# Five mixing products of an encoder block, multiplied by quarters with seven products of sums

## Chip, cores and metric

One core of one Trainium2 chip. The time is that of the device from the start to the end of one execution, in microseconds.

## What is computed

One layer of a hybrid encoder over 512 tokens of width 1024, all in float32. A Mamba-2 branch A and an S5 branch B leave `y_a` (512x1536, before its output matrix) and `y_b` (512x768, before its two). What the change touches is the mixing of the two:

```
A   = y_a @ w_out                                   # 1536 -> 1024
B   = (y_b @ w_glu_a) * sigmoid(y_b @ w_glu_b)      # 768 -> 1024, twice
mix = sigmoid(gate_a) * A + sigmoid(gate_b) * B
h   = LN(alpha * x + mix @ w_o)
out = LN(alpha * h + expert_choice_moe(h))          # 16 experts, 64 tokens each
```

## The kernel before

It is a program with semaphores written by hand, one instruction stream for each engine. The stages follow one another: input projections and gates, S5, the Mamba-2 loop over 4 groups and 4 token tiles, the mixing, the product with `w_o` with the first layer norm and the router, then 8 pairs of experts, whose weights (some 550 MB) stream from HBM.

**The mixing** is done in two halves of 512 output columns, each of three products: m = 0 and 3 with `w_glu_b`, m = 1 and 4 with `w_glu_a`, m = 2 and 5 with `w_out` in two weight slices. A product has four token tiles c (128 tokens); `mix_tile` (L1243) sums one tile in one PSUM bank over 6 (`w_glu`) or 12 (`w_out`) steps of 128 rows, each a matmul of 128x128 weights (tokens) by 512 columns. In float32 each such matmul stands in the trace as two weight loads and two matmul records. Product 0 runs partly inside the Mamba-2 loop; the loop `for m in range(6)` (L1286) runs the rest, 5 products after `y_transposed` of the last tile. `m_bank` (L301) gives products of odd and even m four banks each, so product m waits only for the readers of product m-2 (`before`, L1010).

**Readers.** ScalarE takes products 0 and 3 by tiles through a sigmoid to `sg_u`. VectorE (L1864 to L1882) multiplies products 1 and 4 with `sg_u` and the gate `sg[:, hf, 1]` into `mix`, and products 2 and 5 with the gate `sg[:, hf, 0]` into `tmix`, which it adds to `mix` (`mix_ready`). The gates `sg` come from HBM scratch (L464) once the last tile of branch A is transposed (`yt_copied`).

**After the mixing.** `mix_transposed` (L1302) transposes `mix` by token tiles, ScalarE copies them to `mixT`, `out_product` multiplies by `w_o`, VectorE adds the residual (L1901), and norm, router and the choice of tokens follow, with `max_ready` raised at L1910.

**SyncE's queue** works in the order of the code. `slices` (L391) loads weight slices into a ring of two places, `wring`; slice i waits by `released` for the last reader of slice i-2. In the mixing: slices FIRST_MIX+2.. are `w_out` (two), `w_glu_b`, `w_glu_a`, `w_out` (two), `w_o` (two). Behind them come `x_res` (L467), the first norm's rows `lnrow` (L469), then the expert weights (L471 on), which wait for `mix_ready` 2*TT, for free places of their ring, and (L480) for `max_ready` before they may go over `wring`.

## Time and profile before

| | us |
|---|---|
| median of 3 runs (2117.92 to 2119.32) | 2118.39 |
| the profiled execution | 2114.42 |
| its span in the trace | 2112.7 |
| TensorE busy in the span | 1934.8 (92%) |
| VectorE busy | 589.0 (28%) |
| mean granted TensorE clock | 0.956 of full |

The span is the part of the profiled execution that the trace covers. A share of busy time is a mean over stages with different limits; which engine sets the pace of a stage is read from that stage.

### The profile page before, as it was taken

The page shows a single profiled execution, that of the slowest core. Times are in us where ns is not written, and L with a number is a line of the kernel's source. Part 1 is how long each engine was busy: PE and PEld are TensorE (multiplying, and loading weights), DVE is VectorE, ACT ScalarE, POOL GpSimd, SP SyncE. Part 2 cuts the span into 40 slices and gives each one's busy share as a digit, 9 for nine tenths or more (in the row PEclk, how much of TensorE's full clock was granted, in tenths as well). Part 3 has the DMA queues.
Part 4 walks back from the last instruction along what each step waited for, and adds up shares of the span by engine and source line. Part 5 has one row for each costly group of instructions (what it writes and reads, how often), then busy time and mean ns, then how long its engine had stood idle before and what let it go on. Part 6 is the DMA issues. An engine that isn't in the chain of part 4 may idle for free.

```text
span 2112.7 us, 19729 instructions
## 1 busy us (share of the span) xinstructions
PE 1934.8 (92%) x8256; PEld 913.9 (43%) x8256; DVE 589.0 (28%) x1085; ACT 376.8 (18%) x680; POOL 252.3 (12%) x268
## 2 busy tenths in 40 slices
PE   8999999999999997999898898899888898988987
PEld 4656654466644454343343342343334333334332
DVE  6599757598711134001001001000000100100102
ACT  1444302289700021000000000000000000000001
POOL 1787400165300000000000000000000000000001
PEclk9999999999999998999999999899999999999999
DMA  5632313243332286999999999999999999999995
GB/s 147 137 96 60 106 35 127 70 124 120 105 140 89 88 354 250 418 426 429 427 425 430 428 424 429 428 425 428 428 425 428 429 426 428 427 427 427 429 426 216
DMA packets 92631, 638.13 MB, mean 302 GB/s; under 512 B 21452, under 2 KB 35200, under 8 KB 62336
## 3 DMA queue, kind: packets, MB, share of 16 engines
q1 hardware_dynamic: 79904, 628.99, 73.2%
q10 hardware_dynamic: 12640, 7.89, 1.2%
q8 instruction: 65, 1.06, 0.2%
q14 instruction: 22, 0.18, 0.0%
HBM read 626.98 MB, written 9.88 MB: 301 GB/s over the span
## 4 chain that ended last, share of the span: by engine, by line
PE 59%; DMA 29%; DVE 2%; ACT 2%; issue 0%; SPq 0%; DVEq 0%
PE ps L1000 58%; DMA arena<-in_w_e 29%; ACT arena L663 1%; ACT L663 0%; DVE arena L1925 0%; DVE arena L1923 0%; PE ps L1118 0%; DVE arena L2016 0%; DVE arena L1973 0%; PE ps L1181 0%; PE ps L1492 0%; PE ps L1235 0%; DVE arena L2010 0%; SPq L491 0%; PE ps L1311 0%
## 5 line engine op out<-in xcount | busy, mean ns | idle before, releaser
L1000 PE MATMUL ps<-arena 128*64 128x512 f32 (+8 forms) x7722 | 1869.1, 529 | 144.0 <-DMA arena<-in_w_e 106.7
L1000 PEld LDWEIGHTS ps<-arena 128*64 128x64 f32 (+2 forms) x7722 | 850.4, 162 | 1139.2 <-issue 1035.8
L663 ACT ACTIVATE arena<-ps 128x512 f32<-128x512 f32 (+5 forms) x278 | 152.3, 581 | 1614.6 <-PE ps L1000 916.0
L1982 DVE TENSOR_TENSOR arena<-arena,ps 128x512 f32<-128x512 f32 (+1 forms) x48 | 30.2, 644 | 566.7 <-PE ps L1000 566.6
L655 POOL TENSOR_TENSOR arena<-arena 128x1024 f32<-128x1024 f32 x3 | 7.1, 2352 | 1364.4 <-ACT arena L663 1364.4
L663 ACT ACTIVATE arena<-arena 128x128 f32<-128x128 f32 (+9 forms) x260 | 117.5, 510 | 76.3 <-DVE arena L1889 20.8
L1991 DVE TENSOR_TENSOR arena<-arena,ps 128x512 f32<-128x512 f32 x48 | 33.1, 690 | 335.9 <-PE ps L1000 335.9
L663 ACT ACT_TABLE_LOAD x74 | 94.9, 1283 | 23.0 <-issue 21.3
L1771 DVE SCALAR_TENSOR_TENSOR arena<-arena 128x512 f32<-128x512 f32 x80 | 63.5, 794 | 2.8
L1973 DVE TENSOR_TENSOR arena<-arena 128x512 f32<-128x512 f32 x8 | 5.6, 694 | 185.6 <-PE ps L1492 185.6
L615 POOL TENSOR_TENSOR arena<-arena 128x768 f32<-128x768 f32 x16 | 28.5, 1780 | 180.0 <-PE ps L1181 129.1
L1573 DVE TENSOR_TENSOR arena<-arena 128x320 f32<-128x320 f32 x48 | 28.4, 654 | 0.6
L509 POOL TENSOR_TENSOR arena<-arena 128x256 f32<-128x256 f32 x40 | 24.9, 655 | 4.3 <-ACT arena L663 3.3
L1879 DVE TENSOR_TENSOR arena<-ps,arena 128x512 f32<-128x512 f32 x8 | 5.5, 692 | 71.0 <-PE ps L1000 71.0
L605 POOL TENSOR_TENSOR arena<-arena 128x384 f32<-128x384 f32 x24 | 24.5, 1038 | 3.5 <-PE ps L1000 3.5
L616 POOL TENSOR_TENSOR arena<-arena 128x768 f32<-128x768 f32 x16 | 24.2, 1512 | 0.0
L1871 DVE TENSOR_TENSOR arena<-ps,arena 128x512 f32<-128x512 f32 x8 | 5.5, 691 | 65.4 <-PE ps L1000 38.5
L1458 PE MATMUL ps<-arena 128*128 128x128 f32 x176 | 23.4, 289 | 0.0
L1458 PEld LDWEIGHTS ps<-arena 128*128 128x128 f32 x176 | 21.9, 211 | 3.1 <-DVE arena L1982 3.1
L546 POOL TENSOR_TENSOR arena<-arena 128x512 f32<-128x512 f32 (+4 forms) x19 | 16.8, 886 | 41.9 <-DVE arena L1577 25.3
L647 POOL MEMSET arena<- 128x128 f32 x1 | 0.2, 204 | 176.8 <-PE ps L1311 176.8
L1768 DVE TENSOR_SCALAR arena<-arena 128x512 f32<-128x512 f32 x20 | 10.9, 546 | 36.1 <-ACT arena L663 36.1
(197 smaller groups left out, 686.2 us busy)
## 6 DMA issues: line engine op xcount, KB each, us to landing
arena<-in_w_e SPq DMA_DIRECT2D x120, 2816.0 KB, 28.8
arena<-in_w_e SPq DMA_DIRECT2D x80, 2048.0 KB, 28.4
arena<-in_w_e SPq DMA_DIRECT2D x16, 1408.0 KB, 21.2
arena<-in_w_in SPq DMA_DIRECT2D x9, 2048.0 KB, 8.6
arena<-in_w_e SPq DMA_DIRECT2D x16, 1024.0 KB, 31.3
arena<-cumulative_scratch SPq DMA_DIRECT2D x16, 768.0 KB, 5.1
arena<-in_w_in SPq DMA_DIRECT2D x5, 1536.0 KB, 6.8
arena<-in_w_out_ssd SPq DMA_DIRECT2D x4, 1536.0 KB, 6.7
```

Of the source, the lines that this page charges most:

```text
L509: n.done(eng.tensor_tensor(tmp[t], x, y, ALU.mult))
L546: n.done(pool.tensor_tensor(out[0], x[0], y[0], ALU.mult))
L605: pool.tensor_tensor(xw[:, d].rearrange("p (h w) -> p h w", h=HG), xs[:, c, GI * g:GI * g + GI].rearrange("p (h w) -> p h w", h=HG), last( ...
L615: pool.tensor_tensor(diff_f, cum_rows[:, i % 2, 0], last(cum[:, 0, c, h], P), ALU.subtract)
L616: pool.tensor_tensor(diff_b, cum_rows[:, i % 2, 1], last(cum[:, 1, c, h], P), ALU.subtract).then_inc(s.diff_ready, 1)
L663: return act.activation(out, in_, func, **kw)
L1000: return pe.matmul(out, lhsT, rhs, start=a, stop=z)
L1458: r = pe.transpose(ps[:, i, P * t:P * t + P], block[:, t, :], ident)
L1573: n.done(tt(tv[t], x, y, ALU.mult))
L1771: r = stt(cacc[:, j], raw[:, j, k:k + SEQ], conv_w[:, i, k:k + 1], cacc[:, j], ALU.mult, ALU.add)
L1982: tt(o, o, ps[:, i, 0:w], ALU.mult).then_inc(s.hid_ready, 1)
L1991: r = tt(o, o, ps[:, 6 + k % 2, :], ALU.add)
```

## The change

Product 0 stays as it was. Products 1 to 5 are each cut in quarters: 2x2 quarters of the tokens and the inner dimension on the left (`factors`, a), 2x2 quarters of the inner dimension and the columns on the right (b), 2x2 quarters of 256 tokens by 256 columns in the result. Where eight quarter products would do, seven products of sums are taken: VectorE makes four sums of each side beforehand (`lhs_term`, `rhs_term`), TensorE multiplies P1, P5, P6, P7, P2, P3, P4 (`mix_product`, each in one bank), ScalarE copies P1 to SBUF (`one`), and VectorE adds the seven to the four quarters of the result, in place in the banks (`first_sums`, `last_sum`). Products 1, 3 and 4 have a left side of 768 columns (GK = 3 steps of 128 in a quarter), 2 and 5 one of 1536 (OK = 6). The left sums are made once for `y_b` and once for `y_a`. The 35 products go around eight banks (`product_banks`), so a product waits for the readers of the one eight before it. `mix` and the sigmoid are then made by quarters, in the order of `quarters`. `w_o`'s two slices, and the slice behind each product, are asked for when the last product that reads the place is done, before the last of the seven; `lnrow` and `mixT` hold sums, so `lnrow` is loaded after `mix_ready` TT+3. Transposing of tiles 0 and 1 waits for three quarters, of tiles 2 and 3 for four. Outside the mixing, four semaphores of the S5 parameters (`lr_ready`, `theta_ready`, `tanh_done`, `sin_done`) become two that count to 2, and `before` goes.

```diff
@@ -298,7 +298,43 @@
-        m_bank = ((2, 3, 0, 4), (1, 5, 6, 7))
+        m_bank = (2, 3, 0, 4)
+        product_banks = (1, 5, 6, 7, 2, 3, 0, 4)
+        HALF, GK, OK = SEQ // 2, 3, 6
+        S = Space(arena, ring_at + 11640, top)
+        lhs_glu = S.take(4, GK, HALF)
+        rhs_glu = S.take(4, GK, HALF)
+        rhs_out = [S.take(OK, HALF) for _ in range(2)]
+        flat_rest = lambda x, rest: x.rearrange(rest)[:, OK * HALF:OK * HALF + 2 * HALF].rearrange("p (t w) -> p t w", t=2)
+        with_sixth = S.take(2, HALF)
+        with_fifth, one = flat_rest(mixT, "p a k t -> p (a k t)"), flat_rest(lnrow, "p a d -> p (a d)")
+        rhs_out += [lnrow.rearrange("p a d -> p (a d)")[:, 0:OK * HALF].rearrange("p (k t) -> p k t", k=OK),
+                    mixT.rearrange("p a k t -> p (a k t)")[:, 0:OK * HALF].rearrange("p (k t) -> p k t", k=OK)]
+        S = Space(arena, ring_at - TT * D_MODEL - 2 * 6 - TT * 4 - KT * P, ring_at)
+        lhs_out = [S.take(OK, HALF) for _ in range(2)] + [yT[:, 0:OK, HALF:SEQ], S.take(OK, HALF)]
+        terms_at = lambda m, k: 2 * k if m == 1 else 8 + 4 * (m - 1) + k
+        mix_at = lambda m, n: n if m == 0 else TT + 7 * (m - 1) + n
+        sums_at = lambda m, n: 7 * (m - 1) + n
+        mix_slice = lambda m: FIRST_MIX + m + (m > 2)
+        def factors(m):
+            y, nk, w = (yT, OK, [wring[:, (mix_slice(m) + j) % NW, 0:OK] for j in range(2)]) if m % 3 == 2 else (
+                ysT, GK, [wring[:, mix_slice(m) % NW, GK * j:GK * j + GK] for j in range(2)])
+            a = [[y[:, nk * k:nk * k + nk, HALF * r:HALF * r + HALF] for k in range(2)] for r in range(2)]
+            b = [[w[k][:, :, HALF * q:HALF * q + HALF] for q in range(2)] for k in range(2)]
+            return a, b
+        P1, P5, P6, P7, P2, P3, P4 = range(7)
+        def product(m, x):
+            return ps[:, product_banks[(7 * (m - 1) + x) % 8], :].rearrange("p (t w) -> p t w", t=2)
+        def quarter(buf, r, q):
+            return buf[:, 2 * r:2 * r + 2, HALF * q:HALF * q + HALF]
+        quarters = ((1, 1), (0, 0), (0, 1), (1, 0))
+        quarter_product = (P7, P2, P3, P4)
...
@@ -383,10 +419,14 @@
+                if i == FIRST_MIX:
+                    return s.mix_ps, TT
                 half, j = divmod(i - FIRST_MIX, 4)
+                m = 3 * half + min(j, 2)
                 if j == 2:
-                    return s.slice_used, half + 1
-                return s.mix_ps, TT * (3 * half + min(j + 1, 3))
+                    return s.mix_ps, mix_at(m, 4)
+                sp.wait_ge(s.terms_ready, terms_at(m, 4))
+                return s.mix_ps, mix_at(m, 6)
...
+            sp.wait_ge(s.mix_ready, TT + 3)
             for i, name in enumerate(("ln1_g", "ln1_b")):
...
@@ -898,14 +939,24 @@
-            for half in range(2):
-                m = 3 * half
-                for c in range(TT):
-                    act.wait_ge(s.mix_ps, TT * m + c + 1)
-                    if half:
-                        act.wait_ge(s.mix_read, TT)
-                        act.wait_ge(s.glu_done, TT)
-                    f(sg_u[:, c, :], ps[:, m_bank[m % 2][c], :], ACT.Sigmoid).then_inc(s.mix_sig, 1)
+            for c in range(TT):
+                act.wait_ge(s.mix_ps, c + 1)
+                f(sg_u[:, c, :], ps[:, m_bank[c], :], ACT.Sigmoid).then_inc(s.mix_sig, 1)
+            def first_product_copied(m):
+                act.wait_ge(s.mix_ps, mix_at(m, 1))
+                if m >= 2:
+                    act.wait_ge(s.quarter_sums, sums_at(m - 1, 5))
+                f(one, product(m, P1), ACT.Copy).then_inc(s.one_copied, 1)
+            for m in range(1, 4):
+                first_product_copied(m)
+            act.wait_ge(s.mix_read, TT)
+            act.wait_ge(s.glu_done, TT)
+            for i, x in enumerate(quarter_product):
+                act.wait_ge(s.quarter_sums, sums_at(3, 4 + i))
+                f(quarter(sg_u, *quarters[i]), product(3, x), ACT.Sigmoid).then_inc(s.mix_sig, 1)
+            for m in range(4, 6):
+                first_product_copied(m)
...
@@ -1237,19 +1281,56 @@
+            def mix_tile(c, w):
+                for kk in range(2 * GK):
+                    r = mm(ps[:, m_bank[c], :], ysT[:, kk, P * c:P * c + P], w[:, kk, :], kk == 0, kk == 2 * GK - 1)
+                r.then_inc(s.mix_ps, 1)
+            def taken(m, i):
+                if m == 0:
+                    return s.mix_sig, i + 1
+                return (s.mix_sig, TT + i + 1) if m == 3 else (s.mix_read, TT * (1, 2, 4, 5).index(m) + i + 1)
+            def mix_product(m, x, lhs, rhs):
+                n = lhs.shape[1]
+                for t in range(2):
+                    for k in range(n):
+                        r = mm(product(m, x)[:, t, :], lhs[:, k, P * t:P * t + P], rhs[:, k, :], k == 0, k == n - 1)
+                r.then_inc(s.mix_ps, 1)
+            def mix_products(m):
+                a, b = factors(m)
+                sa, tb = (lhs_out, rhs_out) if m % 3 == 2 else ([lhs_glu[:, j] for j in range(4)], [rhs_glu[:, j] for j in range(4)])
+                slice_wait()
+                if m >= 2:
+                    pe.wait_ge(*taken(max(m - 2, 0), 3))
+                mix_product(m, P1, a[0][0], b[0][0])
+                pe.wait_ge(s.terms_ready, terms_at(m, 1))
+                if m >= 2:
+                    pe.wait_ge(s.one_copied, m - 1)
+                mix_product(m, P5, sa[0], tb[0])
+                pe.wait_ge(s.terms_ready, terms_at(m, 2))
+                if m >= 2:
+                    pe.wait_ge(s.quarter_sums, sums_at(m - 1, 2))
+                mix_product(m, P6, sa[1], tb[1])
+                pe.wait_ge(s.terms_ready, terms_at(m, 3))
+                mix_product(m, P7, sa[2], tb[2])
+                if m % 3 == 2:
+                    slice_wait()
+                pe.wait_ge(*taken(m - 1, 0))
+                mix_product(m, P2, a[0][1], b[1][0])
+                pe.wait_ge(*taken(m - 1, 1))
+                if m == 1:
+                    pe.wait_ge(s.terms_ready, 7)
+                mix_product(m, P3, sa[3], b[1][1])
+                pe.wait_ge(s.terms_ready, terms_at(m, 4))
+                pe.wait_ge(*taken(m - 1, 2))
+                mix_product(m, P4, a[1][1], tb[3])
...
+                    mix_tile(c - (TT - 2), mix_w[0])
+            pe.wait_ge(s.z_silu, GROUPS * TT)
+            pe.wait_ge(s.g_ready, GROUPS * TT)
+            for c in range(2, TT):
+                mix_tile(c, mix_w[0])
+            y_transposed(GROUPS * TT - 1)
+            pe.wait_ge(s.yt_copied, 3 * GROUPS * TT)
+            pe.wait_ge(s.gate_ready, GROUPS * TT)
+            for m in range(1, 6):
+                mix_products(m)
             w_o = []
             def mix_transposed(c):
-                pe.wait_ge(s.mix_ready, TT + c + 1)
+                pe.wait_ge(s.mix_ready, TT + (3 if c < 2 else 4))
                 if c == 0:
-                    pe.wait_ge(*before(4, TT - 1))
+                    pe.wait_ge(s.one_copied, 5)
...
@@ -1861,25 +1937,95 @@
+            def lhs_term(m, k):
+                (a11, a12), (a21, a22) = factors(m)[0]
+                t = lhs_out if m % 3 == 2 else [lhs_glu[:, j] for j in range(4)]
+                x, y, op = ((a21, a22, ALU.add), (t[0], a11, ALU.subtract), (a11, a21, ALU.subtract), (a12, t[1], ALU.subtract))[k]
+                if k:
+                    dve.wait_ge(s.terms_ready, 2 * k if m == 1 else 8 + k)
+                tt(t[k], x, y, op).then_inc(s.terms_ready, 1)
+            def rhs_term(m, k):
+                (b11, b12), (b21, b22) = factors(m)[1]
+                t = rhs_out if m % 3 == 2 else [rhs_glu[:, j] for j in range(4)]
+                x, y = ((b12, b11), (b22, t[0]), (b22, b12), (b21, t[1]))[k]
+                i = mix_slice(m) + (1 if m % 3 == 2 and k else 0)
+                dve.wait_ge(slice_loaded[i % NW], 16 * (i // NW + 1))
+                if k:
+                    dve.wait_ge(s.terms_ready, terms_at(m, k))
+                tt(t[k], x, y, ALU.subtract).then_inc(s.terms_ready, 1)
+            def first_sums(m):
+                dve.wait_ge(s.one_copied, m)
+                dve.wait_ge(s.mix_ps, mix_at(m, 1 + P6))
+                tt(with_sixth, one, product(m, P6), ALU.add).then_inc(s.quarter_sums, 1)
+                dve.wait_ge(s.quarter_sums, sums_at(m, 1))
+                tt(with_fifth, with_sixth, product(m, P5), ALU.add).then_inc(s.quarter_sums, 1)
+                dve.wait_ge(s.mix_ps, mix_at(m, 1 + P7))
+                dve.wait_ge(s.quarter_sums, sums_at(m, 2))
+                tt(with_sixth, with_sixth, product(m, P7), ALU.add).then_inc(s.quarter_sums, 1)
+                dve.wait_ge(s.quarter_sums, sums_at(m, 3))
+                tt(product(m, P7), product(m, P7), with_fifth, ALU.add).then_inc(s.quarter_sums, 1)
+                dve.wait_ge(s.quarter_sums, sums_at(m, 4))
+            def last_sum(m, i):
+                x = quarter_product[i]
+                dve.wait_ge(s.mix_ps, mix_at(m, 1 + x))
+                tt(product(m, x), product(m, x), (one, with_fifth, with_sixth)[i - 1], ALU.add).then_inc(s.quarter_sums, 1)
+                dve.wait_ge(s.quarter_sums, sums_at(m, 4 + i))
+            def taken(m, i):
+                if m % 3 == 0:
+                    return
+                hf, o = m // 3, quarter(mix[:, :, 512 * (m // 3):512 * (m // 3) + 512], *quarters[i])
+                y = product(m, quarter_product[i])
+                if m % 3 == 1:
+                    dve.wait_ge(s.mix_sig, TT if not hf else TT + i + 1)
+                    tt(o, y, quarter(sg_u, *quarters[i]), ALU.mult).then_inc(s.mix_read, 1)
+                    dve.wait_ge(s.mix_read, 2 * TT * hf + i + 1)
+                    tt(o, o, quarter(sg[:, hf, 1], *quarters[i]), ALU.mult).then_inc(s.glu_done, 1)
+                else:
+                    if hf or i:
+                        dve.wait_ge(s.mix_ready, TT * hf + i)
+                    t = tmix.rearrange("p (t w) -> p t w", t=2)
+                    tt(t, y, quarter(sg[:, hf, 0], *quarters[i]), ALU.mult).then_inc(s.mix_read, 1)
+                    dve.wait_ge(s.mix_read, TT * (2 * hf + 1) + i + 1)
+                    dve.wait_ge(s.glu_done, TT * hf + i + 1)
+                    tt(o, o, t, ALU.add).then_inc(s.mix_ready, 1)
+            dve.wait_ge(s.ysT_ready, S5_W // P)
+            for k in range(4):
+                lhs_term(1, k)
+                rhs_term(1, k)
+            dve.wait_ge(s.yt_copied, 3 * GROUPS * TT)
+            for k in range(4):
+                lhs_term(2, k)
+            for m in range(1, 6):
+                first_sums(m)
+                if m == 1:
+                    dve.wait_ge(s.sg_loaded, 64)
+                taken(m, 0)
+                last_sum(m, 1)
+                taken(m, 1)
+                if m in (1, 4):
+                    rhs_term(m + 1, 0)
+                if m == 3:
+                    for k in range(3):
+                        rhs_term(4, k)
+                last_sum(m, 2)
+                taken(m, 2)
+                if m == 2:
+                    for k in range(4):
+                        rhs_term(3, k)
+                last_sum(m, 3)
+                taken(m, 3)
+                if m in (1, 4):
+                    for k in range(1, 4):
+                        rhs_term(m + 1, k)
+                if m == 3:
+                    rhs_term(4, 3)
```

## Rows read from the trace of the kernel before

**Rows 1.** The page: busy time of the engines, chain that ended last by engine
```profile
PE 1934.8 (92%) x8256; PEld 913.9 (43%) x8256; DVE 589.0 (28%) x1085; ACT 376.8 (18%) x680; POOL 252.3 (12%) x268
...
PE 59%; DMA 29%; DVE 2%; ACT 2%; issue 0%; SPq 0%; DVEq 0%
```

**Rows 2.** Chain that ended last, 560 to 840 us: start, us, what
```profile
590.61 144.47 PE ps L1000 x336
...
735.08 0.45 PE ps L1311 x4
...
737.85 13.74 PE ps L1000 x32
```

**Rows 3.** SyncE's queue: longest waits (total, times, longest), then its issues in order
```profile
SPq L480 <- DVE arena L1910: 56.3, 1, 56.3
...
737.50 82.47 SPq L488 DMA_DIRECT2D arena<-in_w_e  x16
...
807.51 12.46 SPq L488 DMA_DIRECT2D arena<-in_w_e  x6
```

**Rows 4.** Two stretches: us, busy PE, PEld, DVE, ACT, POOL, PEclk, DMA share, GB/s
```profile
784.00:807.50 23.50, 21.71 (x88) 12.20 (x87) 16.44 (x45) 7.98 (x12) 0.00 (x0) 1.00 0.01 2
...
807.50:2083.00 1275.50, 1134.52 (x5296) 469.00 (x5298) 90.59 (x152) 73.70 (x139) 0.00 (x0) 0.94 1.00 424
```

**Rows 5.** Groups of TensorE by form, 590.61 to 735.08 us
```profile
L1000 PE MATMUL ps<-arena 128*128 128x512 f32 x336 | 144.5, 592 | 1.0 <-ACT arena L663 1.0
```

**Rows 6.** The weight loads of the same stretch
```profile
L1000 PEld LDWEIGHTS ps<-arena 128*128 128x128 f32 x336 | 63.8, 190 | 81.1 <-issue 79.9 <-ACT arena L663 1.2
```

**Rows 7.** Loads beside 128x384 matmuls, 460.42 to 465.58 us
```profile
L1000 PEld LDWEIGHTS ps<-arena 128*128 128x128 f32 x16 | 3.0, 190 | 2.1
```

**Rows 8.** Matmuls of 128 columns, 934 to 943 us
```profile
L1000 PE MATMUL ps<-arena 128*128 128x128 f32 x64 | 7.9, 284 | 0.9 <-DVE arena L1973 0.9
```

**Rows 9.** Weight loads in order around two 256-column matmuls: start, us, line
```profile
894.29 0.14 PEld L1000 LDWEIGHTS ps<-arena 128*64 128x64 f32 x2 [0.29 <-issue]
...
894.72 0.58 PEld L1000 LDWEIGHTS ps<-arena 128*64 128x64 f32 x6 [0.29 <-issue]
...
895.59 0.14 PEld L1000 LDWEIGHTS ps<-arena 128*64 128x64 f32 x2 [0.29 <-issue]
```

**Rows 10.** VectorE by form, whole span: busy us, mean ns
```profile
L1871 DVE TENSOR_TENSOR arena<-ps,arena 128x512 f32<-128x512 f32 x8 | 5.5, 691 | 65.4 <-PE ps L1000 38.5 <-DMA arena<-gate_scratch 26.9
...
L1719 DVE TENSOR_TENSOR ps<-ps,arena 128x512 f32<-128x512 f32 x12 | 8.4, 700 | 0.4
```

**Rows 11.** VectorE in order, 530 to 640 us
```profile
545.32 0.95 DVE L1798 TENSOR_TENSOR arena<-arena 128x768 f32<-128x768 f32 x1
...
553.90 1.84 DVE L1798 TENSOR_TENSOR arena<-arena 128x768 f32<-128x768 f32 x1
...
577.12 0.42 DVE L1822 TENSOR_SCALAR arena<-arena 128x384 f32<-128x384 f32 x1
...
604.46 0.69 DVE L1871 TENSOR_TENSOR arena<-ps,arena 128x512 f32<-128x512 f32 x1 [26.91 <-DMA arena<-gate_scratch]
```

**Rows 12.** GpSimd in order, 530 to 740 us
```profile
551.05 8.13 POOL L643 COPY arena<-arena 128x512 f32<-128x512 f32 x6
...
736.02 0.20 POOL L647 MEMSET arena<- 128x128 f32 x1 [176.84 <-PE ps L1311]
```

**Rows 13.** DMA issues of 585 to 620 us: count, KB, us to landing
```profile
arena<-gate_scratch SPq DMA_DIRECT2D x4, 1024.0 KB, 8.7
...
arena<-in_w_out_ssd SPq DMA_DIRECT2D x2, 1536.0 KB, 11.2
```

**Rows 14.** DMA issues of the whole span
```profile
arena<-in_w_out_ssd SPq DMA_DIRECT2D x4, 1536.0 KB, 6.7
...
arena<-in_w_o SPq DMA_DIRECT2D x2, 2048.0 KB, 7.9
```

More of the change, by code:

```diff
@@ L691, in _ @@
             f(small[:, 0], par[:, :, 2, :], ACT.Exp).then_inc(s.step_exp, 1)
-            act.wait_ge(s.lr_ready, 1)
-            f(small[:, 3], small[:, 1], ACT.Tanh, scale=0.5).then_inc(s.tanh_done, 1)
-            act.wait_ge(s.theta_ready, 1)
+            act.wait_ge(s.exponent_ready, 1)
+            f(small[:, 3], small[:, 1], ACT.Tanh, scale=0.5).then_inc(s.tanh_sin_done, 1)
+            act.wait_ge(s.exponent_ready, 2)
             f(small[:, 5], small[:, 4], ACT.Sin)
-            f(small[:, 6], small[:, 4], ACT.Sin, scale=0.5).then_inc(s.sin_done, 1)
+            f(small[:, 6], small[:, 4], ACT.Sin, scale=0.5).then_inc(s.tanh_sin_done, 1)
             for c in range(S5_W // P):
@@ L1008, in slice_wait @@
                 return wring[:, i % NW]
-            def before(m, c):
-                sigmoids, products = (0, 3), (1, 2, 4, 5)
-                if m in sigmoids:
-                    return s.mix_sig, sigmoids.index(m) * TT + c + 1
-                return s.mix_read, products.index(m) * TT + c + 1
             pe.wait_ge(s.consts_ready, 7)
@@ L1236, in y_transposed @@
                 r.then_inc(s.yt_ps, 1)
-            nk = 6
             mix_w = []
-            def mix_tile(m, half, c, w):
-                lhs, halves = (yT, 2) if m % 3 == 2 else (ysT, 1)
-                for kk in range(nk):
-                    r = mm(ps[:, m_bank[m % 2][c], :], lhs[:, nk * half + kk, P * c:P * c + P], w[:, kk, :],
-                           half == 0 and kk == 0, half == halves - 1 and kk == nk - 1)
-                if half == halves - 1:
-                    r.then_inc(s.mix_ps, 1)
-                elif c == TT - 1:
-                    r.then_inc(s.slice_used, 1)
+            def mix_tile(c, w):
+                for kk in range(2 * GK):
+                    r = mm(ps[:, m_bank[c], :], ysT[:, kk, P * c:P * c + P], w[:, kk, :], kk == 0, kk == 2 * GK - 1)
+                r.then_inc(s.mix_ps, 1)
@@ L1283, in _ @@
                         mix_w.append(slice_wait())
-                    mix_tile(0, 0, c - (TT - 2), mix_w[0])
-            for m in range(6):
-                if m == 0:
-                    pe.wait_ge(s.z_silu, GROUPS * TT)
-                    pe.wait_ge(s.g_ready, GROUPS * TT)
-                if m == 1:
-                    y_transposed(GROUPS * TT - 1)
-                    pe.wait_ge(s.yt_copied, 3 * GROUPS * TT)
-                    pe.wait_ge(s.gate_ready, GROUPS * TT)
-                for half in range(2 if m % 3 == 2 else 1):
-                    w = slice_wait() if m else mix_w[0]
-                    for c in range(0 if m else 2, TT):
-                        if half == 0 and m >= 2:
-                            pe.wait_ge(*before(m - 2, c))
-                        mix_tile(m, half, c, w)
+                    mix_tile(c - (TT - 2), mix_w[0])
[8 more added lines that the diff above has]
+                mix_products(m)
             w_o = []
             def mix_transposed(c):
-                pe.wait_ge(s.mix_ready, TT + c + 1)
+                pe.wait_ge(s.mix_ready, TT + (3 if c < 2 else 4))
                 if c == 0:
-                    pe.wait_ge(*before(4, TT - 1))
+                    pe.wait_ge(s.one_copied, 5)
                 else:
@@ L1611, in _ @@
             dve.wait_ge(s.step_exp, 1)
[L1612 removed]
+            tt(v(1), a_re, v(0), ALU.mult).then_inc(s.exponent_ready, 1)
             n.link(tt(v(2), a_im, v(0), ALU.mult))
[L1614 to L1616 removed]
+            reduce_phase(v(4), v(2), v(7), v(8), s.exponent_ready)
+            dve.wait_ge(s.tanh_sin_done, 1)
             n.link(ts(v(10), v(3), -1.0, 1.0, ALU.mult, ALU.add))
```

30 lines of the change are left out of this document (4 added, 26 removed).

## The prediction

> **What bounds the kernel now.** I read the page first: TensorE is busy 92% of the span and VectorE 28%, and the chain that ended last is 59% TensorE and 29% waits for DMA [rows 1]. So the place matters more than the share. The chain by time shows the mixing as one unbroken piece: 336 matmul records in 144.47 us from 590.61, then transposes and, from 737.85, the product with `w_o` [rows 2]. VectorE idles most of this stretch. Next, what a shorter mixing moves. SyncE's queue issues the first expert weights at 737.50 and then stands 56.3 us at L480, until L1910 has raised `max_ready` for the last tile, and issues again at 807.51 [rows 3]. The windows show DMA at 2 GB/s from 784 to 807.5 and at 424 GB/s with share 1.00 from there to 2083 [rows 4]. So the expert stage is DMA's, and its start is set by `max_ready`, at the end of TensorE's chain of mixing, `w_o` and router. What the mixing gains before 807.5 reaches the end whole; the first 16 issues were landed 23 us early and cannot hold it back.
>
> **TensorE's part.** Removed: products 1 to 5 at 4 tiles x 6 or 12 steps, two records each: 3 x 48 + 2 x 96 = 336 records of 512 columns [rows 5], 144.47/336 = 0.430 us each. Added: 7 products x 2 token tiles x 3 or 6 steps, two records each: 3 x 84 + 2 x 168 = 588 records of 256 columns, with 588 weight loads in place of 336. A 128x128-weight matmul with 256 columns is not in the trace. Its neighbours: the weight load beside 512 columns takes 190 ns, with 81.1 us of the stretch idle between loads [rows 6]; beside 384 columns 16 loads go by in 5.16 us, 0.3225 each [rows 7], which is three quarters of 0.430, so nothing fixed shows at that width. At 128 columns 64 records take 7.9 us, 0.123 each [rows 8], 0.016 above a quarter of 0.430. With weights of 64 columns, two halves of the array in turn, a burst around the 256-column bank takes 0.87 us from 894.72 to 895.59 for three pairs of loads, where one pair before a 512-column one takes 0.43 (894.29 to 894.72): two pairs of 256 columns in 0.44, 0.22 each [rows 9]. Bounds: half of 0.430 is 0.215 (sum 126.4, gain 18.1); 0.123 plus 128 columns at 0.1075 is 0.231 (sum 135.8, gain 8.7). I take 0.216, near the 384-column row, since 0.216 still leaves a load spaced at 0.123 time to finish: 588 x 0.216 = 127.0 us. **Gain 144.4 - 127.0 = 17.4 us**, if TensorE never waits. A small product is then 12 x 0.216 = 2.6 us, a `w_out` one 5.2 us; product 1 starts at 590.61 as before, 2 at 608.7, 3 at 645, 4 at 663.1, 5 at 681.3, and it ends at 717.5 in place of 734.9.
>
> **VectorE's part, and what hides it.** A 512-element tensor-tensor takes 0.69 to 0.70 us also with banks on both sides [rows 10], 0.72 with the link to the next. 768 elements take 0.95 [rows 11], so 128 elements cost 0.13 and 1536 elements (not in the trace) about 1.75; bounds 1.75 and twice 0.95. With the link: 0.99 and 1.79. The work: sums of factors 16 x 0.99 + 12 x 1.79 = 37 us; 35 sums of products x 0.72 = 25 us; 32 multiplies and adds x 0.72 = 23 us, as before. That is 85 us beside 127. Where it falls decides:
> - The 8 sums of product 1 go where VectorE idles from 577.54 to 604.46 [rows 11]; the `w_glu_a` slice was asked for at 563 and lands in 7. 577.5 + 8 x 0.99 = 585.5, before 590.6. Cost nothing.
> - The 4 left sums of `y_a` start at 590.6, end at 597.8; P6 of product 1 ends at 598.4. Nothing.
> - The gates `sg` land at 604.4 [rows 11], asked for as before. The first quarter waits there. Then 0.72 x 5 to 608.0, the right sum for P5 of product 2 to 609.8, wanted at 613.9. Six steps to 614.1, the right sum for P6 to 615.9, wanted at 619.1. This is the **tightest place, 3.2 us of slack**. That sum also needs the second `w_out` slice: released after P3 of product 1 at 606.2, 6.7 us to landing [rows 14], 612.9.
> - Product 3: its sums start at 642.0 after P3 of product 2 and end at 645.9; P5 wants the first at 647.6, slack 4.6. Product 4: made by 661.6, wanted from 665.7. Product 5: the first at 680.3, wanted 686.4; the second 687.2, wanted 691.6.
>
> Each bank is reused eight products on; its reader is done 7 us or more before, since the readers of a product lag it by 2 to 9 us.
>
> **ScalarE** adds 5 copies of about 0.6 us and makes the second sigmoid by quarters; all in an idle engine, and the P1 copy is ready 2.6 us before P6 ends.
>
> **SyncE's queue.** The slices are asked for one or two products before the end of a stage, earlier against their use than now; the tightest, the first `w_out`, shares DMA with the gates as before (11.2 us, from 592.65) [rows 13], landed about 606.6, wanted 608.7. `w_o`'s second slice, now behind the whole of product 5, comes 5.2 us earlier against its end (2 MB, 7.9 us [rows 14]), so `x_res` stands behind it earlier too. `lnrow` gets a new wait, `mix_ready` TT+3; behind it stand the expert weights, which wait for all eight anyway: P4 ends at 717.5, three steps of 0.72 later, 719.7, against 737.5. Nothing is lost.
>
> **After the mixing.** Tile 0's transposes need three quarters: P3 ends at 712.3, plus 3 x 0.72 = 714.5, under the last product. So they follow TensorE's last matmul at once, as now, and the 70 us from there to `max_ready` stay. The renamed semaphores of S5 move no instruction: nothing.
>
> **Sum.** 2112.7 - 17.4 = 2095.3 us of span, and the profiled execution 2114.42 would be 2097.0. That execution lies 4.0 us under the median of the runs, so the median goes from 2118.4 to **2101.0 us**.
>
> **Rivals.**
> 1. *Short matmuls keep the 128-column row's fixed part.* 0.231 a record: 8.7 us saved, 2109.7. For it: more loads, each hidden under half the columns. Against: the 384-column row has no fixed part and the 64-wide pair only 0.22. Anything between counts here.
> 2. *TensorE waits for VectorE or a slice behind product 1.* If `w_out`'s second slice takes 11.2 us as in the crowded stretch, P6 of product 2 waits 0.1; if linked steps cost 0.3 us more than 0.72, the 13 behind 604.4 take 4 us more and P6 waits 1, and the clock stays up. Price 1 to 5 us: 2102 to 2106.
> 3. *The weight load is not hidden at all.* Then a record would be its columns plus 0.190: 588 x (0.215 + 0.190) = 238 us, 94 slower, 2212. The rows refute it for wide ones: 0.430 would have to be the sum already, and the loads' 63.8 us lie inside TensorE's busy 144.5 [rows 5, 6]. The Trainium skill ("TensorE: Matmul & The Clock Gate", Part 3, "The mechanism") says that a weight load overlaps a running matmul only when the row groups differ; these all use the full 128 rows, so by it every load here would be bare. By that page's figure for a load (ns: columns / 1.2, here 107), the estimate would be 588 x (0.215 + 0.107) = 189 us, 45 slower. This trace disagrees.
> 4. *Slower: VectorE becomes the bound.* GpSimd's copies from 551.05 ran for 8.13 us [rows 12], and the same 768-element instruction took 1.84 under them in place of 0.95 [rows 11], 1.93 times as long. If the VectorE steps of the mixing ran so, the 67 us behind 604.4 (85 less 8, 7 and 3 done by then) become 130: 590.6 + 4 x 3.5 + 4 x 1.4 = 610, + 130 = 740, and with the waits between them TensorE ends near 742 in place of 734.9: 7 us slower, 2125.5. It decides from about 1.8 times on. Against it: GpSimd has no instruction between 559.2 and 736.0 [rows 12]. The Trainium skill ("SBUF — State Buffer", "Who interferes with whom") has such a conflict only between VectorE with two SBUF inputs and GpSimd, and the trace agrees; ScalarE and TensorE run beside.
> 5. *No effect on the end:* were the expert stream not waiting for `max_ready`, the gain would be hidden. The silent 23 us of DMA say no.
>
> **How the numbers follow.** Forecast 0.76; rival 1 0.10; rival 2 0.07; rival 3 0.01; rival 4 0.04; rival 5 0.02. A measurement of this kernel tells 0.2% (4 us) from no change. Forecast, 1 and 2 are faster: 0.93. Same 0.02, slower 0.05. Range: below, the 0.215 bound (2100.3) and 2 us for the spread of executions, 2098.5; above, to rival 1's end, 2110.
>
> **What would show it.** TensorE from 590.6 to about 717.5 without a gap; 588 records near 0.216 us apart; VectorE busy about 75 us in it; first expert issue near 719.7; the second run of issues near 790.1; DMA share 1.00 after it. A gap ahead of P6 of product 2 shows rival 2; loads spaced at 0.23 rival 1; 768-element steps over 1.5 us rival 4. A mixing that ends at 717 with a second issue still at 807 would make the whole argument wrong.

## The result, and the profile after

The changed kernel takes 2101.8 us (median of 4 runs, 2099.09 to 2104.08), the kernel before beside it 2118.86 us (4 runs): a ratio of 0.9918, 95% interval 0.9901 to 0.9935. Measured again with more runs it is 2101.4 us (6 runs) against 2117.71 (17 runs): 0.9918, 0.9906 to 0.9930. The forecast was 2101.0.

The profiled execution of the changed kernel took 2104.08 us, its span is 2102.2. First the page, where [rows 1] stood:

```profile
PE 1915.0 (91%) x8508; PEld 958.2 (46%) x8508; DVE 646.3 (31%) x1148; ACT 379.6 (18%) x685; POOL 251.0 (12%) x268
...
PE 61%; DMA 26%; DVE 2%; ACT 2%; issue 1%; SPq 0%; DVEq 0%
```

TensorE has 252 more matmul records than before and is busy 19.8 us less. VectorE has 63 more instructions, 57.3 us of work; none of the new lines is among the chain's longest pieces. The chain by time, as in [rows 2]:

```profile
595.07 127.43 PE ps L1051 x588
...
724.21 1.06 PE ps L1387 x8
725.27 13.74 PE ps L1051 x32
```

The mixing is one unbroken piece again: 127.43 us in place of 144.47, **17.04 us less**. It starts at 595.07 in place of 590.61, though, so in this pair of profiles its end came only 12.6 us earlier. The groups of TensorE by form in the mixing, for [rows 5, 6]:

```profile
L1051 PE MATMUL ps<-arena 128*128 128x256 f32 x588 | 127.4, 379 | 1.0 <-ACT arena L704 1.0
...
L1051 PEld LDWEIGHTS ps<-arena 128*128 128x128 f32 x588 | 111.4, 190 | 16.9 <-ACT arena L704 1.2
```

588 records at 0.2167 us, with no idle time but the 1.0 us ahead of the first, which the kernel before has too. The loads now fill 111.4 us, but stay beside the matmuls. VectorE in order:

```profile
582.04 0.96 DVE L1946 TENSOR_TENSOR arena<-arena 128x768 f32<-128x768 f32 x1
...
595.05 7.14 DVE L1946 TENSOR_TENSOR arena<-arena 128x1536 f32<-128x1536 f32 x4 [5.59 <-ACT arena L704]
...
608.72 0.69 DVE L1986 TENSOR_TENSOR arena<-ps,arena 128x512 f32<-128x512 f32 x1 [1.54 <-DMA arena<-gate_scratch]
...
612.63 1.76 DVE L1956 TENSOR_TENSOR arena<-arena 128x1536 f32<-128x1536 f32 x1 [0.43 <-DMA arena<-in_w_out_ssd]
...
618.43 5.48 DVE L1956 TENSOR_TENSOR arena<-arena 128x1536 f32<-128x1536 f32 x3
```

A sum of 1536 elements takes 1.76 us, 1.79 from one to the next of the four. The gates landed at 608.7, 13.7 us after the start of the mixing (13.9 before). The two last rows are the tight ones. At 612.63 VectorE waits for the first `w_out` slice, which TensorE wants at 595.07 + 84 x 0.2167 = 613.3: 0.6 us of slack. The first of the three sums at 618.43 is done at 620.2; it is for P6 of product 2, wanted 48 records after 613.3, at 623.7: 3.5 us.

Then SyncE's waits from 590 to 835 us (total, times, longest), and its issues in order, for [rows 3]:

```profile
SPq L521 <- DVE arena L2056: 61.3, 1, 61.3
...
SPq L529 <- DVE arena L2043: 9.6, 1, 9.6
```

```profile
596.91 14.45 SPq L437 DMA_DIRECT2D arena<-in_w_out_ssd  x2
...
724.72 82.67 SPq L529 DMA_DIRECT2D arena<-in_w_e  x16
794.93 12.46 SPq L529 DMA_DIRECT2D arena<-in_w_e  x6
820.64 12.05 SPq L532 DMA_DIRECT2D arena<-in_w_e  x3
```

Counted from the start of the mixing, the second run of issues comes at 199.86 us in place of 216.90: all of the 17.04. The windows of the stretches behind it, as in [rows 4]:

```profile
784.00:794.93 10.93, 9.13 (x52) 6.25 (x50) 8.35 (x28) 4.24 (x7) 0.00 (x0) 1.00 0.00 1
795.00:815.00 20.00, 8.22 (x36) 7.40 (x38) 11.99 (x34) 0.93 (x4) 0.00 (x0) 0.53 0.97 394
815.00:820.00 5.00, 5.00 (x20) 1.65 (x22) 0.00 (x0) 0.00 (x0) 0.00 (x0) 0.85 0.38 159
820.00:2083.00 1263.00, 1127.90 (x5290) 459.67 (x5286) 78.61 (x118) 73.45 (x137) 0.00 (x0) 0.95 0.99 422
```

DMA falls silent once more, in 815 to 820 us (share 0.38): the transfers released by `max_ready` have landed, and the next (L532, 820.64) wait until TensorE's first expert matmuls, from 814.88, have freed a place of the ring. The kernel before has the same hole in front of its issue at L491. So the gate that sets the end is one step behind `max_ready`, and the last experiments go there.

### The profile page after: what moved, and what is told of

It is laid out like the page before. It is cut to its first block, busy times and chain, and to the rows that moved or that the text cites. A ratio compares the mean times of both kernels' runs of the same rounds, so it can differ in the third digit from the quotient of the medians.

```text
span 2102.2 us, 20351 instructions
## 1 busy us (share of the span) xinstructions
PE 1915.0 (91%) x8508; PEld 958.2 (46%) x8508; DVE 646.3 (31%) x1148; ACT 379.6 (18%) x685; POOL 251.0 (12%) x268
## 4 chain that ended last, share of the span: by engine, by line
PE 61%; DMA 26%; DVE 2%; ACT 2%; issue 1%; SPq 0%; DVEq 0%
PE ps L1051 60%; DMA arena<-in_w_e 26%; ACT arena L704 1%; ACT L704 0%; PE ps L1534 0%; DVE arena L2071 0%; DVE arena L2069 0%; PE ps L1162 0%; DVE arena L2162 0%; DVE arena L2119 0%; PE ps L1225 0%; PE ps L1568 0%; DVE arena L2156 0%; PE ps L1279 0%; SPq L532 0%
## 5 line engine op out<-in xcount | busy, mean ns | idle before, releaser
L1051 PEld LDWEIGHTS ps<-arena 128*64 128x64 f32 (+2 forms) x7974 | 896.6, 164 | 1084.1 <-issue 964.0
L1956 DVE TENSOR_TENSOR arena<-arena 128x768 f32<-128x768 f32 (+1 forms) x20 | 25.6, 1278 | 2.6 <-DMA arena<-in_w_out_ssd 1.5
L2139 DVE SCALAR_TENSOR_TENSOR arena<-arena,ps 128x512 f32<-128x512 f32 x8 | 5.5, 690 | 56.0 <-PE ps L1051 56.0
L1801 DVE TENSOR_TENSOR_SCAN ps<-arena,ps 128x128 f32<-128x128 f32 x48 | 19.6, 409 | 0.4
## 6 DMA issues: line engine op xcount, KB each, us to landing
arena<-in_w_e SPq DMA_DIRECT2D x16, 1408.0 KB, 16.3
```

Of the source, the lines that this page charges most:

```text
L1051: return pe.matmul(out, lhsT, rhs, start=a, stop=z)
L1956: tt(t[k], x, y, ALU.subtract).then_inc(s.terms_ready, 1)
```

## The experiments

The kernel before was run beside each. Line numbers in the chain of a kernel shift by the lines it adds.

**1. Was it the early part of the execution?** The kernel before once more, and the changed kernel once more, neither with an edit.

> The kernel before once more, one look, for the same question. Theory A: its mixing starts anywhere from 588 to 597 us, not always at 590.6; the mixing itself is again 144.4 to 144.6 us. Rival (the early part was made longer by the change): 590 to 591.5.

> The changed kernel once more, for the part outside the mixing. In its first profile the mixing starts at 595.07 us, in that of the kernel before at 590.61, and the end came 10.5 us earlier though the mixing is 17.0 us shorter. Theory A: the 4.5 us ahead of the mixing and the 1.8 us behind the first expert matmul are the spread of executions (DMA landings), so this profile starts the mixing elsewhere, between 588 and 597, with the mixing again 127.4 +- 0.3. Rival: the two merged semaphores of the S5 parameters make the early part longer, then the start is again 594.5 to 595.5. Ratio to the kernel before 0.990 to 0.994.

Kernel before: 2122.84 us, mixing from 598.02, 144.47 us. Changed: 2101.4, from 594.97, 127.43. The mixing repeats to 0.01 us. Its start does not: over all the profiles it lies between 590.61 and 598.02, and both ends of that belong to the kernel before. The second profile of the changed kernel alone would have fitted the rival (594.5 to 595.5); what refutes it is that kernels with the changed early part also start at 591.14 (three sums), 591.98 and 592.32 (the plain copies and the second dummy kernel, below), and the kernel before at 598.02. In the first 590 us TensorE idled 23.3 us in the first profile of before, 26.7 in this one and 26.3 in the changed kernel's. So the 4.5 us by which the changed kernel's mixing started later are the spread of executions, not the change; my bound of 588 to 597 for the start was 1 us too narrow.

**2. Only the count of columns.** P1 is multiplied twice, everything else as in the change.

```diff
-                for t in range(2):
+                for t in [0, 1] * times:
...
-                mix_product(m, P1, a[0][0], b[0][0])
+                mix_product(m, P1, a[0][0], b[0][0], 2)
```

> P1 of every product is multiplied twice, so TensorE makes eight quarter products, with everything else of the change in place: the sums, the recombination, the earlier requests for slices and the later one for the norm's rows. Theory (the gain is the count of matmul columns): 5 more products, 84 records, 84 x 0.2167 = 18.2 us: mixing 145.6 us, ratio to the kernel before 1.000 to 1.002. Rival (part of the gain is the earlier requests of w_o, x_res and the norm's rows, or quarters as such): 3 us or more still faster than before, ratio under 0.9985.

2120.9 us (12 runs), ratio 1.0012 (1.0003 to 1.0021). Its TensorE groups in the mixing:

```profile
L1051 PE MATMUL ps<-arena 128*128 128x256 f32 x672 | 145.6, 379 | 1.0 <-ACT arena L704 1.0
```

672 x 0.2167 = 145.6. With eight products the whole gain is gone; what is left of the change (earlier requests, other banks, other order) gains nothing that can be measured. The 1.1 us over 144.47 is the price of records of half the width: 2 x 0.2167 against 0.430, 0.003 us a pair.

**3. Fewer steps still.** P4 takes one of its 3 or 6 steps: this kernel leaves out part of the inner sum of one quarter product.

```diff
-                n = lhs.shape[1]
+                n = steps or lhs.shape[1]
...
-                mix_product(m, P4, a[1][1], tb[3])
+                mix_product(m, P4, a[1][1], tb[3], 1)
```

> P4 sums only the first of its 3 or 6 steps of 128 rows, so one quarter of the result lacks the rest; 64 records less, 3 x 8 + 2 x 20 = 64, 13.9 us at 0.2167. Theory (each us taken from the mixing reaches the end, VectorE has room): mixing 113.6 us, 13.9 us faster than the changed kernel, about 2087 to 2089, ratio to the kernel before 0.985 +- 0.0015. Rival 1 (VectorE is close to its limit and holds TensorE once it is faster): gaps ahead of the first products of the next m and 3 us or more given back. Rival 2 (the expert stream starts by something else): second issue of expert weights moves, the end does not.

2091.08 us (4 runs), ratio 0.9872 (0.9858 to 0.9886). TensorE in order, then two windows:

```profile
593.78 16.70 PE L1051 MATMUL ps<-arena 128*128 128x256 f32 x76 [0.97 <-ACT arena L704]
611.55 97.13 PE L1051 MATMUL ps<-arena 128*128 128x256 f32 x448 [1.07 <-DMA arena<-in_w_out_ssd]
710.07 1.09 PE L1387 MATMUL ps<-arena 128*128 128x128 f32 x8 [1.39 <-DVE arena L1996]
711.99 1.87 PE L1387 MATMUL ps<-arena 128*128 128x128 f32 x8 [0.83 <-ACT arena L704]
```

```profile
711.00:714.00 3.00, 2.17 (x11) 2.03 (x10) 1.04 (x2) 1.55 (x4) 1.06 (x3) 0.68 1.05 403
714.00:717.00 3.00, 3.00 (x6) 1.17 (x5) 0.00 (x0) 1.78 (x2) 0.00 (x0) 0.75 1.05 405
```

Another 10 us come off, so the end still follows TensorE, but 13.9 were expected and a ratio of at most 0.9865. Counted from the start of the mixing, the mixing ends 12.5 us earlier, but the first tile's product with `w_o` only 9.3. Both neighbours show: TensorE waits 1.07 us for the first `w_out` slice, 17.8 us after the start of the mixing, and 1.39 for VectorE's last sums before the transposes, after which the granted clock falls. The 0.68 and 0.75 of the rows are means over both levels; in windows of 1 us it is 0.50 from about 712 to 715.5 us and 1.00 again from 716.

**4. The width of a matmul, by itself.** In the kernel before, products 1, 3 and 4 go in strips of 256 or of 128 columns; the columns stay the same.

```diff
-                for kk in range(nk):
-                    r = mm(ps[:, m_bank[m % 2][c], :], lhs[:, nk * half + kk, P * c:P * c + P], w[:, kk, :],
+                width = 256 if m in (1, 3, 4) else 512
+                for q in range(0, 512, width):
+                    for kk in range(nk):
+                        r = mm(ps[:, m_bank[m % 2][c], q:q + width], lhs[:, nk * half + kk, P * c:P * c + P], w[:, kk, q:q + width],
```

> The kernel before, with the three products of w_glu inside the stretch (m = 1, 3, 4) multiplied in two strips of 256 columns for each token tile: the same number of columns, 288 records in place of 144, no VectorE work added. It prices the narrower matmul by itself. Theory (0.2167 us a record as the changed kernel's 588 in 127.43 show): 3 x 20.6 us becomes 3 x 20.8, 0.5 us in all, ratio 0.999 to 1.001. Rival (a fixed part of 0.016 us a record as the 128-column row has): 288 x 0.231 = 66.5 for 61.9, 4.6 us more, ratio 1.002.

> The same three products in strips of 128 columns: 576 records. Theory: here the weight load sets the pace, since one of 128 columns followed another every 0.11 to 0.123 us in the kernel before: 576 x 0.112 = 64.5 to 576 x 0.123 = 70.8 us for 61.9, 2.6 to 8.9 us more, ratio 1.001 to 1.004. Rival (columns alone set the pace, 0.1075 + 0.0025): under 1.5 us more.

2118.48 us (11 runs), ratio 1.0003 (0.9995 to 1.0012), and 2122.23 (10 runs), 1.0018 (1.0009 to 1.0027). The groups of each:

```profile
L1000 PE MATMUL ps<-arena 128*128 128x256 f32 x288 | 62.6, 379 | 1.0 <-ACT arena L663 1.0
```

```profile
L1000 PE MATMUL ps<-arena 128*128 128x128 f32 x576 | 64.7, 275 | 1.0 <-ACT arena L663 1.0
...
L1000 PEld LDWEIGHTS ps<-arena 128*128 128x128 f32 x768 | 100.7, 191 | 46.7 <-issue 45.4 <-ACT arena L663 1.2
```

0.217 us a record at 256 columns, 0.112 at 128, full clock in both: rival 1's 0.231 is refuted, and with it the reading that 0.123 is a floor. The mixing is 144.83 and 146.99 us long, 0.4 and 2.5 us more than with 512 columns: at 128 columns the low end of what was expected. The last row also says how to read a load. Its 768 loads mix 576 beside 128-column matmuls with 192 beside 512-column ones; between 595 and 611 us, where there are only the former, the mean is 192 ns, while records pass every 112 ns. So a load's duration in the trace is not what it costs; what else it holds is not shown. By a rule of the Trainium skill ("TensorE: Matmul & The Clock Gate", Part 3, "The mechanism"), that a load overlaps only a matmul of other row groups, these full-row loads would stand bare; this trace disagrees at both widths. The same section of the Trainium skill also says that TensorE pulls a load ahead when it goes to the background weight buffer. That would fit, but no run here shows where a load goes.

**5. How much slack VectorE has.** Each right-hand sum of products 2 to 5 is computed twice, then three times.

```diff
+                for _ in range(2 if m >= 2 else 0):
+                    n.link(tt(t[k], x, y, ALU.subtract))
                 tt(t[k], x, y, ALU.subtract).then_inc(s.terms_ready, 1)
```

> Every right-hand sum of products 2 to 5 computed twice. The changed kernel's trace leaves 3.5 us between the end of the sum for P6 of product 2 and its use, and the doubling puts 3.6 us there. Theory: a wait of 0 to 0.4 us ahead of P6 of product 2, no other, the clock stays 1.00, mixing 127.4 to 127.9. Rival (the 32 added instructions of terms_x3 cost in proportion, 9.9 us for 32): 16 of them cost about 5 us.

> Every right-hand sum of products 2 to 5 is computed three times, one after another, 32 VectorE instructions more (16 of 1.79 and 16 of 0.99 us, 44 us), nothing else changed. Theory (VectorE is hidden, and first shows ahead of P6 of products 2 and 5): P6 of product 2 waits some 3 to 4 us, P6 of product 5 some 2 to 3 us, no other gap over 0.5; the mixing 133 to 135 us, 6 to 7.5 us above the changed kernel. Rival (VectorE is spare throughout): no gap, same time. Rival 2 (VectorE is the pace already): all 44 us show.

Twice: 2102.84 us in a single run, mixing 128.2 us where at most 127.9 was expected. Three times: 2112.33 us (6 runs), 0.9974 (0.9962 to 0.9986), mixing 137.4 us where at most 135 was expected. TensorE of each in order:

```profile
594.55 28.82 PE L1051 MATMUL ps<-arena 128*128 128x256 f32 x132 [0.98 <-ACT arena L704]
623.83 98.89 PE L1051 MATMUL ps<-arena 128*128 128x256 f32 x456 [0.47 <-DVE arena L1958]
```

```profile
591.14 28.82 PE L1051 MATMUL ps<-arena 128*128 128x256 f32 x132 [0.97 <-ACT arena L704]
623.67 75.93 PE L1051 MATMUL ps<-arena 128*128 128x256 f32 x336 [3.72 <-DVE arena L1958]
702.03 26.48 PE L1051 MATMUL ps<-arena 128*128 128x256 f32 x120 [2.43 <-DVE arena L1958]
```

The waits fall where the prediction put the tightest place, 132 records in: P6 of product 2, and with three sums also ahead of P6 of product 5, 468 records in. There the waits are 6.15 us, yet the mixing grew by 9.94. The windows behind each wait say where most of the rest went:

```profile
623.60:626.00 2.40, 2.33 (x6) 1.88 (x7) 2.26 (x3) 0.00 (x0) 0.00 (x0) 0.50 0.04 7
...
628.00:630.00 2.00, 2.00 (x6) 1.55 (x6) 1.90 (x2) 0.00 (x0) 0.00 (x0) 0.55 0.00 0
630.00:632.00 2.00, 2.00 (x11) 1.73 (x10) 1.97 (x2) 0.00 (x0) 0.00 (x0) 1.00 0.00 0
...
702.00:704.00 2.00, 1.97 (x9) 1.75 (x10) 1.88 (x2) 0.00 (x0) 0.00 (x0) 1.00 0.00 0
```

Behind the 3.72 us standstill the granted clock is 0.50 (1.2 GHz) for some 6 us, half of which is lost: 3 us. Behind the one of 2.43 it stays at 1.00.

**6. Rival 4, made true.** GpSimd copies SBUF to SBUF beside VectorE: in one kernel 50 plain copies of 768 words, which last only the first 61 us of the mixing, in another 88 reordered ones of 512 words that last the whole mixing. The lines below are of the second. The expert weights in SyncE's queue wait for the last copy.

```diff
+            for i in range(88):
+                if i:
+                    pool.wait_ge(s.maps_cleared, 3 + i)
+                pool.tensor_copy(arena[:, ring_at + 10752:ring_at + 11264].rearrange("p (c s) -> p c s", s=T),
+                                 ysT[:, 0, :].rearrange("p (s c) -> p c s", s=T)).then_inc(s.maps_cleared, 1)
```

> GpSimd copies 768 words a partition 50 times during the mixing, into a place nobody reads, some 2 us each; the expert weights wait for the last copy too. It brings about what the prediction's slower rival needed. Rate theory (a VectorE instruction with two SBUF inputs runs 1.93 times as long under GpSimd): the 1536-element sums take 3.4, the 768-element ones 1.8, the 512-element steps on SBUF 1.3 us; TensorE waits about 1.6 and 3.9 us ahead of P5 and P6 of product 2 and 0.8 ahead of P6 of product 5, the mixing 133.7. Lock theory (such an instruction waits for the end of the running copy, whatever its own length): each gets about the same 1.0 to 1.6 us longer, the 1536-element ones to 2.8 to 3.4 and the 512-element ones to 1.7 to 2.3; mixing 130 to 137. Both: steps with a bank on one side keep 0.69. If nothing of the kind: VectorE as in the changed kernel, mixing 127.4.

> GpSimd copies 512 words a partition 88 times during the mixing, reordered as its copies of 551 to 559 us in the kernel before are (1.35 us each), where the earlier run had contiguous copies (1.22 us for 768 words, and VectorE's instructions with two SBUF inputs only 0.06 to 0.6 us longer). Theory (the 1.84 for 0.95 us of the kernel before came from this kind of copy): 768-element sums 1.7 to 1.9, 1536-element 2.8 to 3.5, 512-element steps on SBUF 1.2 to 1.4 us; P5 and P6 of product 2 wait about 1.6 and 3.9 us, and after the longer wait the clock is 0.50 for some us: mixing 134 to 139 us, ratio to the kernel before 0.995 to 0.998. Rival (as with the contiguous copies): no gap, 127.4 us, ratio 0.992.

2101.51 us (4 runs), 0.9924 (0.9910 to 0.9937), and 2101.69 (4 runs), 0.9920 (0.9906 to 0.9933): no slower than the changed kernel alone, mixing 127.44 and 127.43 us, no wait of TensorE, where both theories on record for the plain copies put 130 to 137 us and the one for the reordered copies 134 to 139. VectorE under the reordered copies, with all 88 from 595.30 to 723.1 us:

```profile
595.27 9.42 DVE L1953 TENSOR_TENSOR arena<-arena 128x1536 f32<-128x1536 f32 x4 [5.60 <-ACT arena L711]
...
608.96 0.69 DVE L1993 TENSOR_TENSOR arena<-ps,arena 128x512 f32<-128x512 f32 x1 [1.41 <-DMA arena<-gate_scratch]
...
612.13 1.26 DVE L1995 TENSOR_TENSOR arena<-arena 128x512 f32<-128x512 f32 x1
613.32 2.63 DVE L1963 TENSOR_TENSOR arena<-arena 128x1536 f32<-128x1536 f32 x1
615.88 0.69 DVE L1982 TENSOR_TENSOR ps<-ps,arena 128x512 f32<-128x512 f32 x1
```

The conflict is there: with two inputs from SBUF, 512 elements mostly take 1.26 in place of 0.69 us (1.8 times; one step took 1.62), 768 take 1.44 to 1.84 in place of 0.96 (1.5 to 1.9), 1536 take 2.44 to 2.63 in place of 1.76 (1.4 to 1.5). Under the plain copies 512 elements mostly take 0.75, 768 take 1.39 to 1.58 and 1536 take 1.93 to 2.37 (1.1 to 1.3 times). A step with a bank among its inputs keeps 0.68 to 0.70. TensorE just escaped a wait: under the reordered copies the sum for P6 of product 2 is done at 623.8 us and wanted 132 records in, at 623.9, so 0.1 us is left of the 3.5.

**7. What stands between `max_ready` and the first free place.** In the changed kernel TensorE stands still twice in the router and its clock is 0.50 from about 796.5 to 816.5 us. Dummy products of 512 columns into a free bank fill its waits: 3 and 7, then 3 and 8 and one more behind the sums of `counts`.

```diff
             affinities_transposed(2)
+            pe.wait_ge(s.wo_read, 2 * TT - 2)
+            busy(3)
             affinities_transposed(3)
+            busy(8)
...
             r.then_inc(s.slot_ps, 1)
+            busy(1)
```

> The changed kernel with ten matmuls of 512 columns (identity by a finished tile, into a bank nobody reads) in the two waits of TensorE for the router's affinities and the choice of tokens: 3 in the wait of 3.1 us, 7 in that of 7.7 us. In the changed kernel the granted clock is 0.50 from about 796 to 815 us, and the two gathers take 3.66 and 3.80 us for 16 records each; the first expert weights that the ring waits for are freed 5.8 us after the first expert matmul. Theory (the clock fell because TensorE stood still, and the expert stream is let go by TensorE's first expert matmuls, not by max_ready): clock 1.00 through the gathers, each under 2.2 us, first expert matmul 3 to 4 us earlier against the end of the w_o product, and the end as much earlier: ratio to the kernel before 0.9895 to 0.9905, where the changed kernel has 0.9918. Rival (the stream is let go by max_ready, as the prediction had it): the gathers are faster and the end is the same. Rival 2: the ten hold the threshold's transpose up, no gain or a loss.

> The changed kernel with three and eight dummy products of 512 columns in TensorE's two waits of the router, and one more between the sums of counts and the first gather. Theory A (the clock fell there because TensorE stood still for 1.4 us more, and the end hangs on the first release of a ring place by the expert matmuls): the gather behind the extra product is granted 1.00 and takes 2.0 us in place of 3.78, the first expert matmul comes some 3.5 us before that of the changed kernel, counted from the start of the mixing, the release at L532 too, and the span is 3.5 us shorter (profile span near 2098.5 for a mixing that starts at 595.0, ratio to the kernel before near 0.9902). Theory B (the end hangs on the rows that DMA delivers, not on when TensorE releases the place): the gather is shorter but the span behind the start of the mixing stays at 1507 us, ratio 0.9918. If the clock falls all the same, the gather stays at 3.8 us, and neither is told apart.

2100.44 us (5 runs), 0.9916 (0.9903 to 0.9930): by its runs not to be told from the changed kernel, where 0.9895 to 0.9905 was expected. The second: 2098.08 (4 runs), 0.9904 (0.9887 to 0.9920), the lowest median of the kernels that compute the whole layer, though its interval overlaps that of the changed kernel. TensorE of the second kernel in order, windows of 1 us, and SyncE's issues:

```profile
801.84 0.22 PE L1462 MATMUL ps<-arena 16*128 16x16 f32 x1 [0.86 <-DVE arena L2109]
802.60 6.43 PE L1051 MATMUL ps<-arena 128*128 128x128 f32 x34 [0.54 <-DVE arena L2113]
809.60 5.62 PE L1051 MATMUL ps<-arena 128*64 128x512 f32 x28 [0.57 <-ACT arena L704]
```

```profile
802.00:803.00 1.00, 0.46 (x5) 0.43 (x4) 0.90 (x3) 0.00 (x0) 0.00 (x0) 1.00 1.00 428
...
805.00:806.00 1.00, 1.00 (x4) 0.46 (x3) 0.67 (x3) 0.00 (x0) 0.00 (x0) 0.50 0.96 406
...
808.00:809.00 1.00, 1.00 (x9) 0.84 (x7) 0.00 (x0) 0.00 (x0) 0.00 (x0) 1.00 0.93 394
```

```profile
792.18 12.29 SPq L529 DMA_DIRECT2D arena<-in_w_e  x6
814.58 7.32 SPq L532 DMA_DIRECT2D arena<-in_w_e  x2
```

Its mixing starts at 592.32. Counted from there, against the changed kernel: the issue behind `max_ready` at 199.86 us in both; the first expert matmul 2.5 us earlier (217.28 against 219.81); the release at L532 3.3 us earlier (222.26 against 225.57); the end of the span 2.8 us earlier (1504.3 against 1507.1). The profile of the first dummy kernel says the same: first expert matmul 1.85 us earlier, release 1.7, end 2.9 (1504.2). The four profiles of the changed kernel without dummies and without a wait in the mixing (both of the changed kernel, both with copies) lie between 1506.7 and 1507.4. So the end moved with the first free place while `max_ready` stood still, as theory A has it, though the two did not move by the same amount. What A said of the clock failed: no gather at 1.00 in 2.0 us, but a clock that fell all the same, at 803.9 us, and came back at 807, with waits of only 0.86 and 0.54 us before it. What the rows show of the gain is that part of the short matmuls ran ahead of that fall, and that the clock was back before the first expert matmul.

## Why the prediction was right, and where it was not

**The main term.** 588 x 0.216 = 127.0 us was forecast, 127.43 measured (0.2167 each); the gain is 17.04 in place of 17.4. Choosing the 384-column row as the nearest was right; the 128-column row misled. Its 64 records follow one another every 0.118 to 0.120 us without a gap, where those of experiment 4 follow every 0.112; why they are slower there is not shown. Experiment 2 shows that this term is the whole effect that can be measured.

**It reaches the end.** Right: the issue behind `max_ready` moved by 17.04 us. The step "its start is set by `max_ready`" was one link short. Behind that gate stand 6 issues with a wait of 9.6 us for `h_ready`, and then the release of a ring place; from the release to the end of the span it takes 1280.4 to 1283.0 us in all fourteen profiles. It changed the number little, since the release stands 97 to 98 us behind the end of the mixing in both kernels (97.07 and 97.38 before, 98.14 and 97.36 after). That the gain "reaches the end whole" does not quite hold in the traces: counted from the start of the mixing the end comes at 1522.1 and 1522.9 us before and at 1507.1 and 1507.4 after, some 15 us earlier and not 17.04. The medians of the runs differ by 17.1 and 16.3. Some 2.0 and 1.5 us are given back; 1.0 and 1.6 us of difference stand behind the release, within the spread just given, and their cause stays open. The missing link also hid a lever, the clock between the two gates.

**VectorE.** 75 us beside the mixing were forecast, 72.2 found. The first eight sums are done 5.6 us ahead of the mixing, where 5.1 was forecast. The slack ahead of P6 of product 2 was put at 3.2 us and is 3.5. But "the tightest place" was not this one. The first `w_out` slice was said to land at 606.6 and to leave 2.1 us; I had placed it where the DMA traffic ends. The semaphore says 15.7 us from the issue, 17.6 after the start of the mixing, which leaves 0.6. The row of 11.2 us [rows 13] is a median of two, one long and one short. Experiment 3 turned that slack into a wait.

**Rivals.** 1 refuted by experiment 4, 3 by the loads hidden at both widths. 2 did not occur; where experiment 5 forced it, "and the clock stays up" was wrong: a wait of 3.7 us costs about 3 more at half clock. 4 did not occur, and experiment 6 shows its price wrong as well: the factor 1.93 was put on every step, but it does not carry over to steps with a bank (1.0) nor in full to long ones (1.5), and what remains fits into VectorE's waits for TensorE, by 0.1 us at the tightest place. I had counted 7 us lost at 1.93 times; the copies cost nothing that can be measured. 5 is refuted by the medians, 17.1 and 16.3 us apart.

**The level.** 2101.0 against 2101.8, with a profile whose early part ran 4.5 us shorter than the changed kernel's. Putting the sum on the median, not on the profiled execution (2097.0 there, 2104.08 measured), is what made it hold. That it holds to 0.8 us is in part luck: the four runs spread over 5 us, the gain was put 0.4 us too high, and what the traces give back behind the mixing was not in the sum.

## What to carry to other kernels

Where TensorE streams fp32 matmuls without a gap, its time is the count of columns to about 1% at 256 columns a matmul, and 4.5% above it at 128 (64.7 us in place of 61.9): seven products for eight is worth its eighth as long as another engine's idle time takes the sums and each operand is ready before its use. Price the slack of each operand by its semaphore, not by the end of its traffic, since a standstill of some us also costs the clock. When a gate is said to set the end, look for the next gate behind it before claiming that it is the last.

## What was not expected of the hardware

- **The clock and a standstill.** 3.72 us of standstill in a full stream: 0.50 for 6 us. 2.43 us: none. Yet 1.39 and 0.83 us with short matmuls between brought 0.50 for about 3.5 us, and 0.86 and 0.54 with one matmul of 16 columns between brought 0.50 for 3 us. The length of one wait does not say it alone; what does was not settled.
- **Matmul width.** 0.430, 0.217 and 0.112 us a record at 512, 256 and 128 columns, each with its own load of 128x128 weights, whose duration in the trace is 190 to 192 ns at all three. In the expert stage of the kernel before, 128-column records stand 0.118 to 0.120 us apart.
- **VectorE beside GpSimd.** With two inputs from SBUF: 1.1 to 1.3 times for a sum of 1536 elements under plain copies, 1.4 to 1.5 for it and mostly 1.8 for a step of 512 under reordered copies. With a bank among the inputs: 1.0.
